# Where the blocks of split activations start in SBUF: 48 and then 64 bytes, instead of 0, 16, 32, 48 and then 64

## Time and profile before

| | |
|---|---|
| three executions | 2650.78, 2656.58 and 2656.96 us; median 2656.58 |
| the profiled execution | 2653.68 us, of which 2652.1 us from its first to its last instruction (the span) |
| TensorE's granted clock, mean over the span | 0.985 of full |
| busy: TensorE, VectorE, ScalarE | 2547.8, 1646.6, 1254.3 us |
| DMA | 579 MB, 218 GB/s on the mean |

### The profile page before, as it was taken

The page is one execution under the profiler, slowest core; times in us unless marked ns, Lnnn a source line. Parts: engine busy times, 40 slices in busy tenths (PEclk is TensorE's granted clock), DMA queues, the critical chain, the costliest instruction groups (busy, mean ns, idle before and its releaser), DMA issues.

```text
span 2652.1 us, 46200 instructions
## 1 busy us (share of the span) xinstructions
PE 2547.8 (96%) x18094; PEld 2376.9 (90%) x18094; DVE 1646.6 (62%) x1911; ACT 1254.3 (47%) x1513; POOL 86.8 (3%) x141
## 2 busy tenths in 40 slices
PE   8999999999889999999999979999799999999997
PEld 7979999999779999999988868978799999997885
DVE  3555466456758777777777764544656666665555
ACT  3454465454454444444444454434555555554443
POOL 0000000000101000000000010000000000000000
PEclk9999999999999999999999989999999999999998
DMA  7445534567647888888877725425345555555552
GB/s 276 177 157 194 191 139 155 193 222 287 251 159 267 323 342 322 348 320 347 345 291 292 275 103 190 159 96 183 135 176 190 191 193 191 192 191 186 195 195 95
DMA packets 79993, 579.04 MB, mean 218 GB/s; under 512 B 8880, under 2 KB 9008, under 8 KB 9776
## 3 DMA queue, kind: packets, MB, share of 16 engines
q1 hardware_dynamic: 64208, 465.60, 47.6%
q0 software_dynamic: 14000, 101.46, 9.9%
q10 hardware_dynamic: 1712, 10.95, 1.1%
HBM read 575.87 MB, written 2.10 MB: 218 GB/s over the span
## 4 chain that ended last, share of the span: by engine, by line
PE 95%; DVE 2%; issue 1%; POOL 1%; ACT 1%; DMA 0%; DVEq 0%; ACTq 0%; POOLq 0%
PE ps L1475 59%; PE ps L1514 25%; PE ps L1479 7%; POOL small L419 1%; PE ps L1440 1%; PE ps L1712 0%; DVE res L1136 0%; DVE xlo L903 0%; DVE xn L1165 0%; PE ps L1575 0%; PE ps L1746 0%; PE ps L1778 0%; PE ps L1757 0%; PE ps L1608 0%; PE ps L1620 0%
## 5 line engine op out<-in xcount | busy, mean ns | idle before, releaser
L885 DVE TENSOR_TENSOR wlo<-raw,whi 128x1024 fp32r<-128x1024 f32 x876 | 1057.7, 1223 | 795.7 <-ACT whi L496 792.1
L496 ACT ACTIVATE whi<-raw 128x1024 fp32r<-128x1024 f32 x876 | 917.6, 1060 | 1038.0 <-PE ps L1475 612.2
L1475 PE MATMUL ps<-xhi,whi 128*128 128x256 f32 x4240 | 1183.5, 279 | 17.5 <-DVE wlo L885 7.7
L1475 PE MATMUL ps<-xlo,whi 128*128 128x256 f32 x4240 | 1179.2, 278 | 0.0
L1475 PE MATMUL ps<-xhi,wlo 128*128 128x256 f32 x4240 | 1178.6, 278 | 0.0
L1475 PEld LDWEIGHTS ps<-xhi,whi 128*128 128x128 f32 x4240 | 799.8, 189 | 19.2 <-issue 11.6
L1475 PEld LDWEIGHTS ps<-xlo,whi 128*128 128x128 f32 x4240 | 800.1, 189 | 0.4
L1475 PEld LDWEIGHTS ps<-xhi,wlo 128*128 128x128 f32 x4240 | 799.9, 189 | 0.0
L1514 PE MATMUL ps<-whi,dhi 128*128 128x512 f32 x704 | 218.2, 391 | 4.1 <-DVE conv L1386 4.1
L911 DVE SCALAR_TENSOR_TENSOR ada<-ada,cb 128x2048 f32<-128x2048 f32 x96 | 219.5, 2286 | 0.0
L1514 PE MATMUL ps<-wlo,dhi 128*128 128x512 f32 x704 | 217.7, 390 | 0.0
(11 more groups left out here) (256 smaller groups left out, 1767.2 us busy)
## 6 DMA issues: line engine op xcount, KB each, us to landing
raw<-in_stream SPq DMA_DIRECT2D x438, 1024.0 KB, 4.8
ada<-in_w_ada POOLq DMA_DIRECT2D x96, 1024.0 KB, 6.6
gamma<-in_ln_g ACTq DMA_DIRECT2D x3, 1024.0 KB, 8.0
beta<-in_ln_b ACTq DMA_DIRECT2D x3, 1024.0 KB, 12.6
mem_nat<-in_mem SPq DMA_DIRECT2D x2, 1024.0 KB, 7.7
res<-in_x SPq DMA_DIRECT2D x1, 2048.0 KB, 21.4
res<-in_x ACTq DMA_DIRECT2D x1, 2048.0 KB, 10.2
out<-xn SPq DMA_DIRECT2D x4, 512.0 KB, 2.7
```

Source lines behind the costliest of these rows:

```text
L496: act.activation(whi[:, h % 4], raw[g % 4][:, 1024 * half:1024 * half + 1024], ACT.Copy)\
L885: dve.tensor_tensor(wlo[:, h % 4], raw[g % 4][:, 1024 * half:1024 * half + 1024], whi[:, h % 4].bitcast(F32), ALU.subtract).then_inc(lo_re ...
L1475: ins = pe.matmul(o, w[:, k, P * m:P * m + P], a(kt), start=begins and n == 0 and m % 2 == 0, stop=ends and n == 2, skip_group_check=True)
```

## The change

`SKEW` gets another list for every one of the six sets. The list has two entries, so block 0 starts 48 bytes behind its place and blocks 1 to 15 start 64 bytes behind. Before, blocks 0 to 3 started 0, 16, 32 and 48 bytes behind, and blocks 4 to 15 64. Readers (`block_of`) and writers (`blocks_of`) both follow the list. The size and the place of every tile stay.

```diff
--- before.py
+++ after.py
@@ -39,7 +39,7 @@
 SHIFT = 64
 APART = 256
 
-SKEW = [(0, 16, 32, 48, 64)] * 6
+SKEW = [(48, 64)] * 6
 
 
 def skew(n, kt):
```

## The result

The kernel after takes 2665.86 us (median of 20 executions, 2649.97 to 2675.67) against 2656.28 us for the kernel before (20 executions on the same chips, 2650.78 to 2658.96). The ratio is 1.0045, with a 95% interval of [1.0035, 1.0056]: slower by 0.45%, where 2645 was forecast. Two things are to be seen. The median is 2 us from that of rival (b), 2664. And the spread has grown from 8 us to 26 us: the fastest execution of the kernel after is 0.8 us faster than any of the kernel before, the slowest 17 us slower.

What follows compares the result with a forecast made beforehand. TensorE's distance between matmul starts on line 1475 was taken as the bound. 58 chunks x 0.19 (11.0 us) plus 0.5 us gave 11.5 off 2656.6, so 2645 us, range 2640 to 2693.

Steps and rivals of the forecast that it cites:

- rival (b): A long stage that starts badly after its layer norm stays slow to its end: +7 us, 2664; chance 0.15.
- Bound, and where to look: TensorE, busy 96% of the span: time follows the distance between matmul starts on line 1475, and little else.
- The two prices, -0.19 and +0.61 us a chunk: Each undisturbed chunk gains 0.19 us if blocks 1 to 15 run at 113.3 ns a matmul, loses 0.61 at 117.8.
- Block 0's 1.42 us: Block 0, moved from 0 to 48 bytes, goes from 1.44 us to the 1.42 block 3 took: 0.02 less.
- The 0.5 us for the chunks among the attention and mLSTM work: gate_a and lstm_o chunks, broken up by attention work, gain about 0.1 us each at blocks 0 to 3.
- The continuity step: A guess: block 0 at 48 bytes, entered from the fast beat, returns to its entry phase and hands the beat on.
- 58 x 0.19: All 58 chunks with an unbroken fast stretch behind their entry stay fast and gain 0.19 us each: 11.0 us.
- the round of 0.473 us: Four matmuls of a block at 48 bytes take 0.473 us; its twelve matmuls are three full rounds.
- No wait ... changes.: No wait, DMA or queue position changes; ScalarE's 612.2 us of idle hide weights being asked for 0.8% sooner.
- Rival (a): Without the block at 0 bytes, the new entry leads into the slow beat everywhere: +35 us, 2692; chance 0.32.
- Rival (c): No effect: the slow entry is each chunk's start-up cost, four blocks long wherever they lie; 2656.6; chance 0.05.
- The range: 2640 to 2693 us for the whole kernel, reaching up to the slow-everywhere case, which holds 0.32.

Runs made afterwards that it cites:

- e10_five_at_48: Kernel after, but with blocks 0 to 3 of every set at 48 bytes and twelve at 64; 2675.3 us, ratio 1.0077 to the kernel before.
- e9_gate_rows_late: Kernel after with the 16 small `gate_rows(1)` matmuls moved from between up2's second and third chunks to behind its last; 2672.28 us, 1.0067 of before.
- e3_all_64: Kernel after without any entry: all 16 blocks of every set at 64 bytes; 2693.59 us, ratio 1.0133 to the kernel before.
- e12_start_later: Kernel after with TensorE's up1 start held until VectorE has written three pairs of xlo blocks instead of two; 2666.28 us, 1.0029 of before.
- e8_mixed_sets: Kernel after with the old entry (0, 16, 32, 48, 64) back in sets 0, 2, 3, 4; sets 1, 5 keep (48, 64); 2649.68 us, 0.9982 of before.

## Why the prediction was wrong

- *Bound, and where to look.* Right. The kernel moved with the distance between starts on line 1475, with the counts of instructions unchanged.
- *The two prices, -0.19 and +0.61 us a chunk.* Right, though 12.0 us / 102 is 117.6 ns and not the 117.8 that was used; the measured slow chunk, 22.62 us, bears out 117.8. In the windows' and the chain's terms: six chunks of qk lost 1.09 us, 0.18 each; twenty of up2 lost 3.72, 0.19 each; up1's 22 gained 13.53, 0.615 each. Block 0's 1.42 us is right too. The 0.5 us for the chunks among the attention and mLSTM work did not come: from the end of qk to the run of 1536 (gate_a) the kernel after took 0.3 us more, and lstm_o took the same.
- *The continuity step.* Right as far as it went. Fast chunks stay fast across the block at 48, in qk, gate_b and up2, and across four such blocks in e10_five_at_48. It had been called the weak step, and for the fast beat it held. For the slow beat it has the two exceptions above.
- *"58 x 0.19", all chunks fast.* This is the step that failed. What the step had to show was not only that the entry hands the fast beat on, but that each stage is in it. Continuity says as much of the slow beat as of the fast one: the round of 0.473 us returns to the phase at which it was entered, whichever that is. The runs bear this out but for those two turns. The forecast took one half of that rule and put the other half, as rival (b), at 0.15. In the profile of after 30 chunks are fast and 27 slow (of these one of q_idx, q_mem, 22 of up1, lstm_q, lstm_k and the second of up2), and one q_idx chunk is disturbed by the clock. 30 x -0.19 + 27 x 0.61 = +10.8 us in place of the forecast's -11.0. Between the two spans it is +15.4, of which the two falls of the clock make 4.4; that leaves +11.0. Between the medians it is +9.6.
- *Rival (b)* named the mechanism, the size of the main part (13.4 forecast, 13.53 found) and the total (2664, found 2665.86). That the total fits so well is in part luck: it had all other 36 chunks fast, and five of them were slow in the profile. Its evidence was on the table: the one slow chunk of up2, mended by the entry after it. What that row says is that the kernel before starts some stages in the slow beat and relies on the entry to leave it; the short entry was judged by whether it would disturb a fast chunk, while the job of the long one was to repair a slow one.
- *"No wait ... changes."* Wrong in one place. A TensorE that is 0.17 us ahead at block 4 of up1's first chunk has to wait for a half of `wlo`, which is there in time for the kernel before. The wait itself costs 0.06 us and would be nothing, if the slow beat of the 22 chunks did not begin there. That the turn comes at this gap is seen in three profiles (after, e9_gate_rows_late and e3_all_64). That the gap causes it is not shown: taking the gap away (e12_start_later) did not settle whether up1 is then fast.
- *Rival (a)* did not come, but its time did, in the experiments that leave a block at 0 and cut the ramp. Its mechanism, that the lack of the block at 0 leads there, fits e3_all_64 but not the kernel after, where 30 chunks are fast without that block; the surer way is that block without the full ramp behind it.
- *Rival (c)* falls in the kernel after, whose block 1 takes 1.36 us in qk, where (c) has four slow blocks; and by e3_all_64, where no ramp at all costs 1.3% instead of nothing. The page that the prediction cites ("TensorE: Matmul & The Clock Gate" of the Trainium skill, "Part 2: What happens when you issue a matmul") states that TensorE reads moving operand and weights through two independent ports. It says nothing of where an operand lies; that the place would not matter was the prediction's reading. Whether the ports are independent is not tested by any run here.
- *The range and the spread.* The range, 2640 to 2693, held the time. Not foreseen was that the answer is a distribution: 8 us of spread became 26, most likely because a stage's beat is drawn in each execution.

Open: what in the chip makes the two beats; why the full ramp alone of seven lands fast; why a kernel without a ramp is slow nearly everywhere; what sets the two slow chunks apart that the short entry turned fast; with what chance a pause hands over the one or the other. Single stages' draws in the executions that were not profiled are inferred from their times, not seen. Of the 2.4 us more between the starts of q_mem and of up1, 0.7 is q_mem's slow beat (22.94 us for its run) and 1.7 the fall of the clock in the cross attention.

## What to carry to other kernels

When a part of a start-up costs a little at every repetition, ask what state it restores before you ask what it costs: here 0.19 us a chunk bought a reset, and where a stage begins badly without it each of its chunks takes 0.61 us more. A rule that says "what comes in goes out" must be read for the bad state too, and the state in which each long stage begins has to be read from the profile, at its first chunk. Take the cheap entry only in the stages whose start is seen to be good, as e8_mixed_sets does, and judge it by the spread of many executions, not by one profile.

## What was not expected of the hardware

- The same 12 matmuls at the same addresses take 1.36 or 1.41 us (113.3 or 117.8 ns each), and which of the two is kept for up to 22 chunks, 498 us, once it is taken up. In up1's first chunk the turn from fast to slow was seen at a weight load that came 0.07 us late (0.13 in e3_all_64).
- The reach of it goes beyond the tensors that were moved: in e9_gate_rows_late the run of 1536, half of whose matmuls read `ohi` and `olo`, which lie where they always did, took 6.2 us more than in the kernel after, 0.78 for each of its 8 chunks. The whole step from fast to slow is 0.61 + 0.19 = 0.80 a chunk, so the matmuls on `ohi` and `olo` must have changed with the others.
- Entries with a block at 0 are the most regular of all (spreads of 0.5 to 5 us on two to four executions) and the slowest, unless 16, 32 and 48 follow.
- The granted clock after the same 2.95 us of idle time was 1.00 in one execution and 0.50 in another, which is worth 2.7 us in the q_idx stage.
